# Moving a layer's DMA additions one layer earlier, and reordering the end of each down product

## The reference

```
x = LN(a*x + conformer_conv(x));  x = LN(a*x + ffn(x) + sigmoid(x Wg)*(p Wp))           # first
x = LN(a*x + stick_breaking_attention(x) Wo);  x = LN(a*x + ffn(x) + sigmoid(x Wg)*(p Wp)) # second
x = x + 0.5*rms(swiglu(rms(x)))                                                           # third
x = x + rms(hybrid_mixer(rms(x)) Wout);  x = x + 0.5*rms(swiglu(rms(x)))                  # fourth
ffn(x)    = (silu(conv3(x W_gate)) * (x W_up)) W_down     # 1024 -> 2816 -> 1024
swiglu(x) = (silu(x W_gate) * (x W_up)) W_down
```

## Time and profile before

| | |
|---|---|
| median of three runs | 2264.41 us |
| profiled execution, its time | 2263.4 us |
| its span, first to last instruction | 2261.8 us |
| TensorE busy | 2195.7 us, 97% |
| VectorE, ScalarE, GpSimd busy | 1644.0, 1199.5, 720.7 us (73%, 53%, 32%) |
| chain that ended last | PE 75%, DVE 10%, ACT 6%, DMA 5%, issue 2% |
| DMA | 350.75 MB, q1 (SyncE, ScalarE) 32.0%, q0 (GpSimd) 19.3% of the engines' time |

### The profile page before, as it was taken

The page is one execution under the profiler, slowest core; times in us unless marked ns, Lnnn a source line. Parts: engine busy times, 40 slices in busy tenths (PEclk is TensorE's granted clock), DMA queues, the critical chain, the costliest instruction groups (busy, mean ns, idle before and its releaser), DMA issues.

```text
span 2261.8 us, 37043 instructions
## 1 busy us (share of the span) xinstructions
PE 2195.7 (97%) x13094; PEld 1886.0 (83%) x13094; DVE 1644.0 (73%) x2447; ACT 1199.5 (53%) x2126; POOL 720.7 (32%) x482
## 2 busy tenths in 40 slices
PE   8999999999999999999999999999899999999998
PEld 6767898888888787899987899988778768899986
DVE  6966656678744345766698888888658972899898
ACT  6665444456655545443465644456645674444475
POOL 6944444321236535322102322221112343311101
PEclk9999999999999999999999999999999999999999
DMA  6636465675458864332264256695354593223364
GB/s 207 197 117 246 147 154 140 152 209 192 159 198 170 193 237 139 118 102 97 98 214 163 75 139 145 144 244 189 136 190 150 123 148 93 101 96 110 102 223 144
DMA packets 117497, 350.75 MB, mean 155 GB/s; under 512 B 12496, under 2 KB 12496, under 8 KB 117328
## 3 DMA queue, kind: packets, MB, share of 16 engines
q1 hardware_dynamic: 76320, 242.91, 32.0%
q0 software_dynamic: 36928, 92.29, 19.3%
q10 hardware_dynamic: 4144, 14.16, 1.9%
HBM read 338.76 MB, written 94.37 MB: 191 GB/s over the span
## 4 chain that ended last, share of the span: by engine, by line
PE 75%; DVE 10%; ACT 6%; DMA 5%; issue 2%; POOL 1%; DVEq 0%; SPq 0%; ACTq 0%; POOLq 0%
PE banks L953 9%; PE banks L955 8%; PE banks L954 8%; PE banks L1162 5%; PE banks L1164 5%; PE banks L1163 5%; PE banks L1251 4%; PE banks L1253 4%; PE banks L1252 4%; DMA raw<-ws 4%; PE banks L1296 3%; PE banks L1298 3%; PE banks L1297 3%; PE banks L986 2%; PE banks L988 2%
## 5 line engine op out<-in xcount | busy, mean ns | idle before, releaser
L1849 ACT ACTIVATE wH<-raw 128x1024 fp32r<-128x1024 f32 x363 | 380.9, 1052 | 419.3 <-DMA raw<-ws 138.5
L690 POOL TENSOR_TENSOR wL<-raw,wH 128x1024 fp32r<-128x1024 f32 x110 | 282.4, 2572 | 447.5 <-ACT wH L1849 444.0
L953 PE MATMUL banks<-xH,wH 128*128 128x512 f32 (+1 forms) x1080 | 413.4, 383 | 11.4 <-DVE xL L2587 7.4
L954 PE MATMUL banks<-xL,wH 128*128 128x512 f32 (+1 forms) x1080 | 407.8, 378 | 0.0
L955 PE MATMUL banks<-xH,wL 128*128 128x512 f32 (+1 forms) x1080 | 407.7, 377 | 0.0
L953 PEld LDWEIGHTS banks<-xH,wH 128*128 128x128 f32 x1080 | 203.7, 189 | 57.0 <-DVE wL L2592 8.5
L955 PEld LDWEIGHTS banks<-xH,wL 128*128 128x128 f32 x1080 | 203.6, 188 | 38.0
L954 PEld LDWEIGHTS banks<-xL,wH 128*128 128x128 f32 x1080 | 203.9, 189 | 35.4
L853 POOL TENSOR_TENSOR wL<-raw,wH 128x1024 fp32r<-128x1024 f32 x36 | 100.6, 2796 | 187.0 <-ACT wH L1849 187.0
L1162 PE MATMUL banks<-wH,mixXH 128*128 128x512 f32 x312 | 122.8, 393 | 12.0 <-DVE mixXL L2996 7.0
L1163 PE MATMUL banks<-wH,mixXL 128*128 128x512 f32 x312 | 121.5, 389 | 0.0
(11 more groups left out here) (416 smaller groups left out, 6230.4 us busy)
## 6 DMA issues: line engine op xcount, KB each, us to landing
raw<-ws SPq DMA_DIRECT2D x327, 512.0 KB, 3.3
raw<-sums SPq DMA_DIRECT2D x44, 512.0 KB, 4.2
sums<-ws POOLq DMA_DIRECT2D x20, 1024.0 KB, 6.4
firsts<-ws POOLq DMA_DIRECT2D x44, 256.0 KB, 5.0
sums<-firsts POOLq DMA_DIRECT2D x44, 256.0 KB, 5.8
thirds<-ws POOLq DMA_DIRECT2D x44, 256.0 KB, 6.3
sums<-sums POOLq DMA_DIRECT2D x44, 256.0 KB, 5.7
raw<-ws SPq DMA_DIRECT2D x44, 256.0 KB, 3.3
```

Of the source, the lines that this page charges most:

```text
L690: pool.tensor_tensor(wL[:, j, :], raw[:, j, :], fp(wH[:, j, :]), ALU.subtract).then_inc(low_ready, 1)
L953: pe.matmul(bank, wH[:, slot, cols], rh, start=start, stop=False)
L954: pe.matmul(bank, wH[:, slot, cols], rl, start=False, stop=False)
L1849: act.activation(high_slot(c)[:, 0:w], raw_slot(c)[:, 0:w], ACT.Copy).then_inc(high_ready, 1)
```

## The change

GpSimd's additions for layer 2 are issued in layer 1's gate-and-up loop, by the code that issues layer 0's in layer 0's loop (`of = 2 * inst`). Those of the first pair of feature tiles (and the second pair's first sum) are issued ahead of the loop, between splits (`first_pair_sums`). The loops of layers 2 and 3 now hold no additions. Of layer 0's twelve copies four are issued at once after the convolution, the others after the splits of chunks 24, 26, 28, 30 and 32 to 35. At the end of each down product the high and the sum of the last part go ahead of the high and low of chunk `X_AT[8]`, and the table load of ScalarE goes last. The low of chunk 0 of the down product goes ahead of the last gate product. The highs of the next layer's first two chunks come after the statistics of two blocks (of layers 0 to 2), no longer before.

```
 def first_pair_sums(inst, begun):                    # new
     split(begun ...);      bases_there(inst); first_sum(inst, 0); third_sum(inst, 0)
     split(begun + 1 ...);  second_sum(inst, 0); first_sum(inst, 1)
     split(begun + 2 ...);  fourth_sum(inst, 0)
...
 # plain_splits, PAIRED 2 (layers 2 and 3): only the lows of the last sums are left
-                        first_sum(inst, 0, t)
-                        fourth_sum(inst, -1, t)
                         low_of_last_sum(u, 1, t)
-                        second_sum(inst, 0, t)
-                        third_sum(inst, 0, t)
                         low_of_last_sum(u, 2, t)
 # plain_splits, PAIRED 1 (layers 0 and 1)
+                of = 2 * inst
                 with pool.Fori(0, count - 2) as t:
                     round_there(1, t)
-                    second_sum(inst, 1, t)
-                    third_sum(inst, 1, t)
+                    second_sum(of, 2, t)
+                    third_sum(of, 2, t)
                     low(cp + 8, t)
-                    first_sum(inst, 2, t)
-                    fourth_sum(inst, 1, t)
+                    first_sum(of, 3, t)
+                    fourth_sum(of, 2, t)
                     low(cp + 9, t)
...
 # GpSimd's order
+                if inst == 0:
+                    copy_at = [SLOTS + 2 * n for n in range(4)] + [3 * SLOTS + n for n in range(4)]
+                    for n in range(4):
+                        copy_base(0, n)
+                    for i in range(4 * SLOTS):
+                        split(begun // SLOTS, begun % SLOTS)
+                        if i in copy_at:
+                            copy_base(0, 4 + copy_at.index(i))
+                        begun += 1
...
+                    first_pair_sums(0, begun)
...
+                    first_pair_sums(2, begun + 1)     # inst 1, behind layer 2's copies
...
 def layer_norm(name, xname, shift, following):        # ScalarE, layer 0 -> attention
     c = CHUNK[following]
+                unit_block(name, 0)
+                unit_block(name, 1)
+                high(c)
                 high(c + 1)
-                for q in range(3):
-                    unit_block(name, q)
+                unit_block(name, 2)
...
 def down_highs():                                     # ScalarE
                     chunk(Y_AT[10])
-                    act.preload_act_table_set("natural_log_exp_and_others")
+                    parts_high(NP + 10)
                     chunk(X_AT[8])
                     chunk(X_AT[9])
-                    parts_high(NP + 10)
                     chunk(X_AT[10])
-                    if inst < 3:
-                        high(d0 + DOWN)
+                    act.preload_act_table_set("natural_log_exp_and_others")
...
 # ScalarE, layer 1 -> layer 2
-            high(CHUNK["gateup2"] + 1)
             deviation("down1", 0)
             deviation("down1", 1)
+            high(CHUNK["gateup2"])
             pre_block("down1", "ff1_pre", 0)
+            high(CHUNK["gateup2"] + 1)
             pre_block("down1", "ff1_pre", 1)
 # post_and_pre: the same for layer 2 -> mixer; "wout" -> layer 3 keeps its order
...
 # VectorE, seven_h and paired_h, in the last pass
                     dve.tensor_tensor(h[:, HALF[0]], ..., w, ALU.add).then_inc(seven_sum, 1)
+                    if last:
+                        low_of_chunk(0)
                     dve.wait_ge(seven_sum, ...)
                     dve.tensor_tensor(h, h, ..., ALU.mult).then_inc(h_made, 1)
 # VectorE, down()
-                    low_of_chunk(0)
...
-                    low_of_chunk(X_AT[8])
-                    parts(NP + 10, X_AT[9])
+                    parts(NP + 10, X_AT[8])
+                    low_of_chunk(X_AT[9])
                     low_of_chunk(X_AT[10])
```

More of the change, by code:

```diff
@@ L798, in sums_of_step, with first_pair_sums @@
                     fourth_sum(inst, j - 2)
+            def first_pair_sums(inst, begun):
+                split(begun // SLOTS, begun % SLOTS)
+                bases_there(inst)
+                first_sum(inst, 0)
+                third_sum(inst, 0)
+                split((begun + 1) // SLOTS, (begun + 1) % SLOTS)
+                second_sum(inst, 0)
+                first_sum(inst, 1)
+                split((begun + 2) // SLOTS, (begun + 2) % SLOTS)
+                fourth_sum(inst, 0)
             def plain_splits(inst):
@@ L806, in plain_splits @@
                     low_of_last_sum(u, 0, 0)
[L807 to L822, removed]
                     low_of_last_sum(u, 1, 0)
-                    tile_there(2)
-                    second_sum(inst, 0)
-                    third_sum(inst, 0)
                     low_of_last_sum(u, 2, 0)
                     with pool.Fori(1, count - 1) as t:
-                        tile_there(1, t)
-                        first_sum(inst, 0, t)
-                        fourth_sum(inst, -1, t)
                         low_of_last_sum(u, 1, t)
-                        tile_there(2, t)
-                        second_sum(inst, 0, t)
-                        third_sum(inst, 0, t)
                         low_of_last_sum(u, 2, t)
-                    tile_there(1, count - 1)
-                    first_sum(inst, count - 1)
-                    fourth_sum(inst, count - 2)
                     low_of_last_sum(u, 1, count - 1)
[L841 to L848, removed]
                     return
@@ L854, in low @@
                         .then_inc(low_ready, 1)
[L856 to L862, removed]
                 def round_there(k, t=0):
@@ L866, in round_there @@
                     pool.wait_ge(raw_loaded[c % SLOTS], t * 16 + 16 * LOADED[c])
-                bases_there(inst)
-                first_sum(inst, 0)
+                of = 2 * inst
                 round_there(0)
-                second_sum(inst, 0)
-                third_sum(inst, 0)
+                second_sum(of, 1)
+                third_sum(of, 1)
                 low(cp + 4)
-                first_sum(inst, 1)
-                fourth_sum(inst, 0)
+                first_sum(of, 2)
+                fourth_sum(of, 1)
                 low(cp + 5)
@@ L878, in plain_splits @@
                     round_there(1, t)
-                    second_sum(inst, 1, t)
-                    third_sum(inst, 1, t)
+                    second_sum(of, 2, t)
+                    third_sum(of, 2, t)
                     low(cp + 8, t)
-                    first_sum(inst, 2, t)
-                    fourth_sum(inst, 1, t)
+                    first_sum(of, 3, t)
+                    fourth_sum(of, 2, t)
                     low(cp + 9, t)
                 round_there(count - 1)
[L886 to L891, removed]
+                second_sum(of, NP - 1)
+                third_sum(of, NP - 1)
+                fourth_sum(of, NP - 1)
             def down_parts(inst):
@@ L914, in _ @@
             for inst in range(3):
-                if inst < 2:
+                if inst == 0:
[3 more added lines that the diff above has]
+                    for i in range(4 * SLOTS):
+                        split(begun // SLOTS, begun % SLOTS)
+                        if i in copy_at:
+                            copy_base(0, 4 + copy_at.index(i))
+                        begun += 1
+                    begun += 1
+                    split((begun - 1) // SLOTS, (begun - 1) % SLOTS)
+                    first_pair_sums(0, begun)
+                    begun += 3
+                if inst == 1:
                     for n in range(COPIES):
                         split(begun // SLOTS, begun % SLOTS)
-                        copy_base(inst, n)
+                        copy_base(1, n)
                         begun += 1
-                if inst == 1:
                     for n in range(NP + 2):
@@ L928, in _ @@
                         begun += 1
+                    split(begun // SLOTS, begun % SLOTS)
+                    first_pair_sums(2, begun + 1)
+                    begun += 4
                 splits(begun, CHUNK[f"gateup{inst}"] + 2 * SEVEN_FROM[inst] + (2 if PAIRED[inst] == 1 else 0))
@@ L2403, in post_and_pre @@
             def post_and_pre(name, xname, following):
-                high(CHUNK[following] + 1)
+                c = CHUNK[following]
+                if name == "wout":
+                    high(c + 1)
                 post_block(name, 0)
                 post_block(name, 1)
+                if name != "wout":
+                    high(c)
                 pre_block(name, xname, 0)
+                if name != "wout":
+                    high(c + 1)
                 post_block(name, 2)
```

## The result

The kernel after took **2244.79 us** (median of 5 runs, 2243.29 to 2246.48), the kernel before 2263.63 beside it: ratio 0.9913, 95% interval 0.9900 to 0.9927, so 0.9% faster. The profiled execution took 2246.48 us, its span is 2244.5 against 2261.8. Predicted were 2246.

What follows compares the result with a forecast made beforehand. The prediction took the kernel to be bound by TensorE, with a few microseconds movable at each of a dozen places. Its terms summed to -18.0 us, from 2263.4 to 2245.4 (2246.4 from the median): 2246 predicted, range 2238 to 2255.

Steps and rivals of the forecast that it cites:

- Third loop -8.5: Layer 2's gate-and-up loop, freed of additions, takes as long as the fourth: 180.0 to 171.5 us.
- its down start -4.0: Layer 2's down product no longer waits for additions; its start takes 63.0 us like the fourth's, not 67.0.
- Second loop +3.2: Layer 1's loop takes in the additions and pays what the first loop shows: 191.8 against 188.6 us.
- The rival that contention is conserved: The second loop pays 8.5 us instead of 3.2; total -12.7, 2251.7 us; chance 12 in 100.
- Layer 0's copies -4.0: Spreading the twelve copies speeds the load at 173.84 us that held ScalarE: -4.0 us, ends 0 and -5.4.
- The bound of 5.4: Most that layer 0's spread copies can win: squares started at 183.34, their statistic was ready at 177.95 us.
- Layer 1's end -2.4: Second to third layer: statistics ahead of the highs start the squares 3.8 us earlier; net -2.4 us.
- layer 2's -2.1: Third layer to the mixer: squares start 4.0 us earlier, less 1.9 for two highs: -2.1 us.
- the 1.45: TensorE's 1.45 us wait for the second turning matrix after layer 2, expected to stay or fall.
- Layer 0's end +0.8: First layer to attention: the first high comes later, so GpSimd's low and the product do too: +0.8 us.
- Down starts 2 x -0.43: First two layers' down products: chunk 0's low comes in time, saving only VectorE's 0.43 us idling each: -0.9 us.
- Last parts -0.1 at the kernel's end alone: Down products' ends: the last part's low comes 0.3 to 0.4 us earlier, leaving -0.1 at the kernel's end.

Runs made afterwards that it cites:

- e1: Kernel before with only layer 2's additions moved into layer 1's loop, layer 0's copies and all end orders as before: 2255.38 us, ratio 0.9966.
- e5: Kernel before with layer 2's additions, in its own loop, over 16 of 128 rows: 2256.37 us, executed once.
- e7: Kernel after with the copies for layer 2 kept out of the stretch where the sigmoid projection's loads land: 2243.40 us, ratio 0.9899.
- e8: Kernel after with both highs ahead of the block statistics again where layer 0 ends: 2246.17 us, ratio 0.9910.
- e4: Kernel after with layer 2's additions inside layer 1's loop over 16 of 128 rows: 2241.75 us, ratio 0.9911.
- e6: Kernel after with the four additions of a round issued together in the loops of layers 0 and 1: 2241.14 us, ratio 0.9888.
- e2: Kernel before with only the new places of layer 0's twelve copies: 2259.66 us, ratio 0.9981.
- e3: Kernel before with only the orders of ScalarE and VectorE changed, GpSimd's order as before: 2258.39 us, ratio 0.9980.

## Why the prediction was right, and where its terms were off

- **Third loop -8.5, its down start -4.0.** Measured -8.6 and -4.0, and shown to be the additions' bytes (e1, e5). But one profile did not fix these prices: with the additions in place that loop took 180.0, 178.7 and 178.7 us, the down start 67.0, 64.3 and 67.5. Over these the terms are -7.7 and -3.3. The chain ran through a late load eight times in that loop, not ten; ten is the number of TensorE's waits. The price does not hang on it.
- **Second loop +3.2.** The term that was furthest off in size. The first layer's one profile, 191.8 - 188.6, was taken as the price. The profile after paid 5.5, e1 3.8, e7 2.8, e8 4.0: mean 4.0. The first loop with the same code spans 189.8 to 192.7 in nine profiles, mean 191.0, a price of 2.4, where the prediction took 3.2. The forecast's condition, a second loop near 193 and well below 197, held (194.1).
- **The rival that contention is conserved** (8.5 in the second loop) falls: none of four came above 5.5. The rule of the Trainium skill (DMA: Bandwidth & Descriptors, "Issuing engines are not separate DMA queues"), that DMAs of all engines share the same DMA engines and interleave, agrees with the landings and with e4 and e5. That equal bytes then cost equal time does not follow from it: in e6 they cost 0.
- **Layer 0's copies -4.0.** -4.8, and e2 shows it to be this part alone; the load took 4.71 us, inside 3.5 to 5.3. The bound of 5.4 was the squares' head start; over all profiles the stage gives 4.0 to 5.6. Whether the clock has a part in it stays open: it fell to 0.5 for 3.41 us in this stage of the kernel before (at 203.5 us) and not in that of the kernel after. The two old-order profiles with a fall at 203.5 take 131.7 and 131.8 us, one with a fall at 188.6 takes 130.9 and one with none 131.0.
- **Layer 1's end -2.4, layer 2's -2.1.** -2.3 and -2.0 when the last part's 0.4 is counted by itself, and e3 shows them to come from the orders alone. Layer 1's number is right in part by luck. Its first turn starts 3.1 us earlier (52.37 instead of 55.45 after the stage's start); behind it the wait for the second turn (0.87) and one for VectorE's `xL` (0.83) take some back, and up to 1.4 us come from the clock, which the prediction leaves out. In all four traces with the old order the granted clock falls to 0.5 within 0.6 us of the end of the wait for the first turn, which lasted 3.1 to 4.2 us, and the stage takes 65.9, 65.9, 66.8 and 67.9 us; in the eight with the new order it stays 1.00 and the stage takes 63.2. So the price was 2.6 to 4.7 us. In the stage after layer 2 the clock stayed 1.00 before and after. There the first wait, of 2.44 us, went; the 1.45 did not stay or fall but rose to 2.15, since its turn got earlier by 2.4 and TensorE came to it earlier by 3.1.
- **Layer 0's end +0.8.** +0.6 (and back -0.5 in e8), with the low of GpSimd as the thing waited for, as worked out.
- **Down starts 2 x -0.43.** -0.5 each, the wait moved to the next step; e3 is the one kernel in which layer 0's did not come.
- **Last parts -0.1 at the kernel's end alone.** Measured -0.4 in each of the four products, -1.6 in all. The step that only the last one shows in the sum was wrong: the earlier low moves TensorE 0.4 us earlier in every product. VectorE's later end was already paid for in the ends' own terms, and at the kernel's end it cost nothing: from the ledger's last matmul to the end it is 17.46 us before and 17.43 after.
- **Not in the sum:** the convolution, untouched, took +2.0. In the twelve profiles that stage took 112.1 to 116.7 us, at a granted clock of 1.00, and nearly all of the spread arises in its first 8 us; why stays open.

The stages with a term sum to -18.3 (forecast -18.0); with the others, +2.0 - 1.1 + 0.3 - 0.2, the ledger gives the span's -17.3. That it is so near is in part luck: a second loop 2.2 dearer than forecast is offset by 0.8 at the copies and 1.5 at the last parts, and up to 1.4 us of layer 1's end came from a cause that the prediction did not name.

## What to carry to other kernels

A transfer that runs beside a tuned loop is not paid by its bytes as such but by the one load on which the round waits: find that load and issue the extra transfers right behind it. It may be worth trying before the work is moved to another stage; no run here tried it in the third loop, so whether the move was needed stays open. Measure a stage between the same two matmuls of both traces. A stage that waits for DMA, or in which TensorE's clock falls, needs more than one profile before its price goes into a sum. Look at the granted clock behind every long wait of TensorE: what ends the wait may give back more than the wait.

## What the hardware showed that was not expected

- A stage in which nothing waits for a transfer can repeat almost exactly from run to run (the second loop's stage is 197.56 us in eight traces: four kernels without additions there, e4, and the three with them at the head of the round), while stages that do wait for loads beside GpSimd's transfers spread over 3 to 4 us (the first loop 189.8 to 192.7, the stretch from 831 to 858 us 25.3 to 28.9). Having no GpSimd transfers is not enough: the convolution at the start, with none and changed by no kernel here, took 112.1 to 116.7, and layer 1's end in its old order 65.9 to 67.9.
- The granted clock fell to 0.5 for 3.41 or 6.83 us at a few places inside the kernel. What that costs can be read at layer 1's end: the same 32 turning matmuls took 4.07 us at 1.00 (after), 5.43 with 3.41 us at 0.5 (before) and 6.76 with 6.83 us at 0.5 (e1).
- An eighth of the bytes is not an eighth of the landing: additions of 32 KB took 2.3 to 3.1 us (e4), those of 256 KB 4.5 to 6.0 in the same loop of the kernel after.
